# The modulation sums of a two-block layer: partition sums by 64 TensorE transposes, or by VectorE block transposes, column sums and five products

## The reference

```python
silu_c = jax.nn.silu(c)                 # (1, 2048)
silu_cc = jax.nn.silu(c_ctx)            # (2048,)
mod = (silu_c @ w_ada[l] + b_ada[l])    # w_ada: 2048 x 12288
mod_c = silu_cc @ w_ada[l] + b_ada[l]
sh_a, sc_a, gt_a, sh_f, sc_f, gt_f = split(mod, 6)      # 2048 values each
csh_a, csc_a, ...                    = split(mod_c, 6)  # only the first two are used
h  = rms_norm(x, g_attn) * (1 + sc_a) + sh_a            # hc likewise, for the context
x  = x + gt_a * mixer(h, hc)
h  = rms_norm(x, g_ffn) * (1 + sc_f) + sh_f
x  = x + gt_f * swiglu(h, ...)
```

## Time and profile before

| | |
|---|---|
| median of 3 runs | 2425.29 us (2425.19 to 2425.72) |
| profiled execution | 2426.32 us |
| its span, first to last instruction | 2424.6 us |
| mean granted TensorE clock | 0.999 |
| TensorE busy (matmuls) | 2402.5 us, 99% |
| VectorE busy | 1800.6 us, 74% |
| ScalarE busy | 1119.0 us, 46% |
| GpSimd busy | 162.2 us, 7% |
| moved by DMA | 556.93 MB, mean 230 GB/s |

### The profile page before, as it was taken

One profiled execution on the slowest core, in us unless ns is written; L12 is line 12 of the kernel. 1 busy time (PEld: TensorE's weight loads), 2 busy tenths in 40 slices (PEclk: granted clock), 3 DMA queues, 4 the chain that ended last, 5 costly groups with the idle time before them and its releaser, 6 DMA issues.

```text
span 2424.6 us, 28710 instructions
## 1 busy us (share of the span) xinstructions
PE 2402.5 (99%) x11098; PEld 1977.9 (82%) x11098; DVE 1800.6 (74%) x2429; ACT 1119.0 (46%) x1464; POOL 162.2 (7%) x186
## 2 busy tenths in 40 slices
PE   9999999999999999999999999999999999999998
PEld 7888888888888888888788888777788888888887
DVE  5688868888899888788878857677777765555555
ACT  5344444444455454456743333644544443444443
POOL 2010000000000001000011100002000100000000
PEclk9999999999999999999999999999999999999999
DMA  9888766666588668877985656455898976667663
GB/s 303 256 269 273 239 218 195 195 184 195 188 267 267 211 213 292 293 257 255 316 270 186 222 171 233 132 159 177 268 302 283 292 233 193 195 211 227 210 213 124
DMA packets 280100, 556.93 MB, mean 230 GB/s; under 512 B 18503, under 2 KB 23901, under 8 KB 278428
## 3 DMA queue, kind: packets, MB, share of 16 engines
q1 hardware_dynamic: 270588, 515.16, 66.0%
q0 software_dynamic: 9088, 37.85, 5.4%
q10 hardware_dynamic: 288, 2.10, 0.2%
HBM read 543.07 MB, written 15.11 MB: 230 GB/s over the span
## 4 chain that ended last, share of the span: by engine, by line
PE 94%; DVE 3%; issue 1%; ACT 1%; DMA 1%; SPq 0%; POOL 0%; ACTq 0%; POOLq 0%; DVEq 0%
PE pb L2155 92%; PE pb L2159 3%; DVE wlo L1395 1%; DMA raw<-in_w_in 1%; DVE acc L1417 1%; ACT whi L939 0%; DVE sm L1946 0%; DVE x L1774 0%; DVE across L1427 0%; DVE gn L2015 0%; DVE x L1777 0%; DVE x L1495 0%; DVE stz L1497 0%; DVE x L1510 0%; DVE fl L2003 0%
## 5 line engine op out<-in xcount | busy, mean ns | idle before, releaser
L939 ACT ACTIVATE whi<-raw 128x1024 fp32r<-128x1024 f32 (+1 forms) x791 | 828.2, 1049 | 1105.5 <-PE pb L2155 1030.5
L1395 DVE TENSOR_TENSOR wlo<-raw,whi 128x1024 fp32r<-128x1024 f32 (+1 forms) x791 | 958.1, 1218 | 446.8 <-ACT whi L939 444.6
L2155 PE MATMUL pb<-whi,xh 128*128 128x512 f32 (+1 forms) x1184 | 465.1, 393 | 0.7 <-DVE xl L1548 0.7
L2155 PE MATMUL pb<-whi,xl 128*128 128x512 f32 (+1 forms) x1184 | 458.2, 387 | 0.0
L2155 PE MATMUL pb<-wlo,xh 128*128 128x512 f32 (+1 forms) x1184 | 457.6, 386 | 0.0
L1417 DVE SCALAR_TENSOR_TENSOR acc<-raw,silc,acc 128x512 f32<-128x512 f32 x480 | 346.1, 752 | 5.7 <-DMA raw<-in_w_ada 0.7
L2155 PE MATMUL pb<-whi,fh 128*128 128x512 f32 x704 | 274.8, 390 | 1.4 <-DVE fl L2003 1.4
L2155 PE MATMUL pb<-whi,fl 128*128 128x512 f32 x704 | 274.0, 389 | 0.0
L2155 PE MATMUL pb<-wlo,fh 128*128 128x512 f32 x704 | 273.9, 389 | 0.0
L2155 PEld LDWEIGHTS pb<-whi,xh 128*128 128x128 f32 x1184 | 222.6, 188 | 46.6 <-issue 2.9
L2155 PEld LDWEIGHTS pb<-whi,xl 128*128 128x128 f32 x1184 | 222.3, 188 | 46.0
(11 more groups left out here) (426 smaller groups left out, 2828.9 us busy)
## 6 DMA issues: line engine op xcount, KB each, us to landing
raw<-in_w_in SPq DMA_DIRECT2D x375, 512.0 KB, 4.6
raw<-in_w_ada SPq DMA_DIRECT2D x192, 512.0 KB, 4.9
raw<-in_ffn_wg SPq DMA_DIRECT2D x88, 512.0 KB, 4.4
raw<-in_ffn_wu SPq DMA_DIRECT2D x88, 512.0 KB, 4.8
raw<-in_ffn_wd SPq DMA_DIRECT2D x88, 512.0 KB, 4.1
raw<-in_w_branch SPq DMA_DIRECT2D x64, 512.0 KB, 3.9
raw<-in_w_out SPq DMA_DIRECT2D x64, 512.0 KB, 4.4
scr_h<-sil POOLq DMA_DIRECT2D x11, 512.0 KB, 4.0
```

Of the source, the lines that this page charges most:

```text
L939: return eng.activation(dst, src, ACT.Copy)
L1395: tt(wlo[:, u, a:b, 0:n], raw[:, l % NRAW, a:b, 0:n], f32(whi[:, u, a:b, 0:n]), ALU.subtract) \
L2155: return eng.matmul(dst, l, r, start=start, stop=stop)
```

## The change

Each slot is now summed by itself. VectorE transposes `acc[:, slot]` in place in blocks of 32 x 32, so that `acc[32 a + i, 32 j + r]` becomes what stood in partition 32 a + r, column 32 j + i, and reduces over r into 16 columns of a new tile `part` [128, 256]: `part[32 a + i, j]` is the sum over the 32 partitions of quarter a. This is done one beat after the piece's end (`fold`, now a chain of VectorE, ahead of the `ada_end` chains and behind the others), for the second row of pieces 0 to 7 two beats after. The four quarters are added on TensorE by one product with `kfold`, a constant 128 x 128 matrix of 16 unit matrices of 32, which leaves the sum on all four quarters. There are five groups: pieces 0 to 7 (256 columns of `part`), and four times four pieces (64 columns). The product comes six beats after the group's last piece (five for the group of piece 19), and VectorE then picks from each quarter of the PSUM bank every fourth column and adds the bias, in four small ops a group. `across` goes, GpSimd's `fold` goes, and GpSimd loads `kfold` (64 KB) after the rope tables.

```diff
--- before.py
+++ after.py
@@ -111,6 +111,7 @@
         co, si = np.cos(ang), np.sin(ang)
         return np.stack([np.concatenate([co, co], -1), np.concatenate([-si, si], -1)], 1).astype(np.float32)
 
+    c["k_fold"] = np.tile(np.eye(32, dtype=np.float32), (4, 4))
     c["k_rope128"] = rope(128)
     c["k_rope64"] = rope(64)
     return c
@@ -184,7 +185,8 @@
         ident = small("ident", [128, 128])
         par = small("par", [128, 112])
         mod = small("mod", [128, 8, 16])
-        across = small("across", [128, 512])
+        part = small("part", [128, 256])
+        kfold = small("kfold", [128, 128])
         bcol = small("bcol", [128, 96])
         rope_off = small_at[0]
         ropeA = small("ropeA", [128, 2, 2, 128])
@@ -528,8 +530,11 @@
 
 
 
-        pairs = [[(p, 0), (p, 1)] for p in range(8)] + [[(p, 0), (p + 1, 0)] for p in range(8, len(pieces), 2)]
-        pair_of_piece = {p: f for f, pair in enumerate(pairs) for p, _ in pair}
+        groups = [range(8)] + [range(p, p + 4) for p in range(8, len(pieces), 4)]
+
+        def part_of(p, m):
+            rows, n = pieces[p][1], pieces[p][2]
+            return 16 * (4 * rows[m] + n if p < 8 else p - 8)
 
         def sub_done(i):
             s, _, _, end = subs[i]
@@ -593,6 +598,8 @@
         B["h2"] = E["o3"], E["o3"] + 2
         B["gT"] = [ada_beat[11] + 9, ada_beat[23] + 9]
         B["gta"] = B["ot"][7] + 2
+        B["ada"] = [ada_beat[g[-1]] + 6 for g in groups]
+        B["ada"][3] = ada_beat[19] + 5
         B["hid"] = [E[f"fu{s}"] for s in range(11)]
 
         GAP = dict(na=5, gq=4, ml=3)
@@ -736,13 +743,6 @@
                               scr_row.rearrange("h x -> (h x)").partition_broadcast(128)) \
                     .then_inc(*M.inc(S("scr_band"), "scr_band", by=16))
 
-            def fold():
...
-
             def ln_rows(key, b, k, g, bias):
                 yield from until(b)
                 W.wait_ge("exb_free", k - 1)
@@ -770,6 +770,7 @@
                 eng.dma_start(ropeB[:, :, :, :].rearrange("p t a b -> p t (a b)"),
                               I["k_rope64"].rearrange("(t p) a b -> p t (a b)", p=128)) \
                     .then_inc(*M.inc(S("rope_in"), "rope", by=16))
+                eng.dma_start(kfold[:, :], I["k_fold"]).then_inc(*M.inc(S("kfold_in"), "kfold", by=16))
                 for i, n in enumerate(("gqa_gq_2", "gqa_gk_2", "diff_gsub_2")):
                     eng.dma_start(grow[:, i, :], I[n][0].partition_broadcast(128)) \
                         .then_inc(*M.inc(S("grow_in"), "grow", i, by=16))
@@ -917,7 +918,7 @@
                             .then_inc(*M.inc(S("hs_in"), "hs", s, a, by=16))
 
             chains = [start(), na_table(), band_table(), ln_rows("ln_b", B["ln_b"], 1, "sgu_ln_g", "sgu_ln_b"),
-                      ln_rows("ln_d", B["ln_d"], 3, "conv_ln_g", "conv_ln_b"), tables(), attention1(), residual(), fold(),
+                      ln_rows("ln_d", B["ln_d"], 3, "conv_ln_g", "conv_ln_b"), tables(), attention1(), residual(),
                       context(), norm1(), gqa(), mla1(), out2(), gates(), norm2(), hidden(), final(), na_bias(), diff()]
             for i in range(NSUB + 2):
                 beat[0] = i
@@ -1401,10 +1402,11 @@
                 W.wait_ge("raw", l)
                 if x == 0:
                     W.wait_ge("silc")
-                    if pair_of_piece[p]:
-                        W.wait_ge("across", pair_of_piece[p] - 1, 2)
-                        if 1 in slots[p]:
-                            W.wait_ge("ada_sum", pair_of_piece[p] - 1)
+                    for m in range(two):
+                        if 0 < p < 8:
+                            W.wait_ge("folded", p - 1, m)
+                        elif p >= 8:
+                            W.wait_ge("folded", *((7, p - 8) if p < 10 else (p - 2, 0)))
                     if p == 0:
                         W.wait_ge("relT")
                 for k in range(2):
@@ -1417,38 +1419,38 @@
                             ins = stt(a, raw[:, l % NRAW, k, :], c, a, ALU.mult, ALU.add)
                         ins.then_inc(*M.inc(S("ada_acc"), "ada", p, x + k, m))
                 M.value["raw_free", l] = M.value["ada", p, x + 1, two - 1]
-                f = pair_of_piece[p]
...
-                        tt(dst, dst, bcol[:, col:col + 4], ALU.add).then_inc(*M.inc(S("mod"), "mod", r, n))
+
+            def fold():
+                for p in range(len(pieces)):
+                    for m in range(len(pieces[p][1])):
+                        yield from until(ada_beat[p] + 1 + m)
+                        a, k = acc[:, slots[p][m], :], part_of(p, m)
+                        W.wait_ge("ada", p, 15, m)
+                        eng.transpose(a, a).then_inc(*M.inc(S("ada_t"), "turned", p, m))
+                        W.wait_ge("turned", p, m)
+                        if p == 8:
+                            W.wait_ge("ada_sum", 0)
+                        eng.tensor_reduce(part[:, k:k + 16], a.rearrange("p (j r) -> p j r", r=32), AX, ALU.add) \
+                            .then_inc(*M.inc(S("ada_fold"), "folded", p, m))
+
+            def ada_end(g):
+                yield from until(sum_beat[g] + 1)
+                W.wait_ge("ada_sum", g)
+                for a in range(4):
+                    q = slice(32 * a, 32 * a + 32)
+                    if g == 0:
+                        sums = side("ada_sum", g)[q, 0:256].rearrange("p (t c m a) -> p t c m a", t=2, c=2, m=16)
+                        bias = bcol[q, 0:32].rearrange("p (c m) -> p c m", c=2).unsqueeze(1).broadcast_to([32, 2, 2, 16])
+                        dst = mod[q, 0:4, :].rearrange("p (t c) m -> p t c m", t=2)
+                        tt(dst, sums[:, :, :, :, a], bias, ALU.add).then_inc(*M.inc(S("mod"), "modq", g, a))
+                    else:
+                        c0, (r,), _ = pieces[groups[g][0]]
+                        sums = side("ada_sum", g)[q, 0:64].rearrange("p (m a) -> p m a", a=4)
+                        tt(mod[q, r, :], sums[:, :, a], bcol[q, c0 // 128:c0 // 128 + 16], ALU.add) \
+                            .then_inc(*M.inc(S("mod"), "modq", g, a))
+                for p in groups[g]:
+                    for r in pieces[p][1]:
+                        M.value["mod", r, pieces[p][2]] = M.value["modq", g, 3]
 
             def evacuate(s, tb):
                 kind, n, ps = s.evac[0], s.ncols, main_ps(s, tb)
@@ -2111,7 +2113,7 @@
                       *[oT_low("ml", h, B["ml"][h] + 4) for h in range(4)],
                       ot_low(), gates(), norm2(),
                       hidden(), final(),
-                      *[ada_end(f) for f in range(len(pairs))]]
+                      fold(), *[ada_end(g) for g in range(len(groups))]]
             for i in range(NSUB + 2):
                 beat[0] = i
                 for s in strips:
@@ -2491,16 +2493,17 @@
                         W.wait_ge("mod", row, n)
                     tr(ps[0:16, 0:128], mod[:, row, :]).then_inc(*M.inc(S("side"), "gT", r))
 
-            def ada_sum(f):
-                yield from until(ada_beat[pairs[f][1][0]] + 4)
+            def ada_sum(g):
+                yield from until(B["ada"][g])
                 while min(busy.values()) > beat[0]:
                     yield
-                sum_beat[f] = beat[0]
...
-                ins.then_inc(*M.inc(S("side"), "ada_sum", f))
+                sum_beat[g] = beat[0]
+                last = groups[g][-1]
+                W.wait_ge("folded", last, len(slots[last]) - 1)
+                W.wait_ge("kfold")
+                ps = take(("ada_sum", g), ("modq", g, 3), beat[0] + 1)
+                a, n = (0, 256) if g == 0 else (64 * g - 64, 64)
+                mm(ps[:, 0:n], kfold[:, :], part[:, a:a + n]).then_inc(*M.inc(S("side"), "ada_sum", g))
 
             mlw = (("Tc", "mkn", 3), ("Tc", "mqr", 3), ("Tc", "mqn", 3), ("kpT",))
             chains = [small_start(), mixer(), rows_T(("yT", "A"), B["yA"], a_in, ("yl", "A"), ("grp", 3)), sgu(),
@@ -2535,7 +2538,7 @@
                                lambda c, h=h: k4[:, c, h, 128:256], ("oTl", 8 + h), *mlw) for h in range(4)],
                       gates(),
                       h2_T(),
-                      *[ada_sum(f) for f in range(len(pairs))]]
+                      *[ada_sum(g) for g in range(len(groups))]]
             def warm(n):
                 for _ in range(n):
                     mm(banks[NMAIN - 1][:, 0:128], ident[:, :], ident[:, :])
```

More of the change, by code:

```diff
@@ L737, in band_table @@
                     .then_inc(*M.inc(S("scr_band"), "scr_band", by=16))
-            def fold():
-                for f, pair in enumerate(pairs):
-                    yield from until(ada_beat[pair[1][0]] + 1)
-                    W.wait_ge("across", f, 2)
-                    eng.tensor_tensor(acc[:, 1, :], acc[:, 1, :], across[:, :], ALU.add) \
-                        .then_inc(*M.inc(S("folds"), "fold", f))
             def ln_rows(key, b, k, g, bias):
@@ L1419, in ada @@
```

(11 more changed lines are left out.)

23 lines of the change are left out of this document (removed).

## The result

| | before | after |
|---|---|---|
| median of 5 runs each | 2425.19 us (2424.87 to 2425.72) | 2416.5 us (2415.61 to 2417.49) |
| profiled execution | 2426.32 us | 2416.5 us |
| span | 2424.6 us | 2414.8 us |
| mean granted clock | 0.999 | 0.999 |

The ratio is 0.9964, 95% interval 0.9950 to 0.9977: 8.7 us faster, for a forecast of 9.2 us and 2416.1. The span fell by 9.8; the profiled execution of the kernel before lay 1.1 us above its median, that of the kernel after on it, so 8.7 is the gain and 9.8 the sum of what the two traces show.

What follows compares the result with a forecast made beforehand. TensorE bounds the kernel, busy 2402.5 of 2424.6 us. Gains 6.66 + 0.3 - 0.67 + 1.6 + 1.3 = 9.2 us, taken off 2425.29, give 2416.1; range 2413.8 to 2419.8.

Steps and rivals of the forecast that it cites:

- Transposes removed: TensorE's queue: fifteen of the sixteen four-transpose sums go, at 0.44 us each, 6.66 us gained.
- The other price: Skill page's 275 ns for each of 64 transposes on TensorE: 17.5 us, forecast near 2407; not used for the sum.
- rival 4: Some of the 16 transpose blocks on TensorE were free; half of 6.66 would give 2419.4; chance 0.03.
- The small wait for GpSimd: TensorE's smaller wait for GpSimd's fold, at the first one-row pair's sum, goes: 0.3 us gained.
- Products added: Five `kfold` products on TensorE, one of 256 columns and four of 64: 0.67 us lost, ends 0 and 1.1.
- The folds at no cost: VectorE's folds of 1.4 us after the 24 pieces cost TensorE nothing; 4.2 us for three without cover.
- Rival 3: VectorE becomes the bound where already full, folds delaying low halves and raw loads; 2430; chance 0.03.
- The stalled stretch: Piece 19, from 1661.33 to 1665.62: TensorE stands 2.7 us instead of 4.29, 1.6 us gained.
- Rival 2: The stalled stretch's stand doesn't shrink because GpSimd holds up VectorE's ops, fold included; 2419.2; chance 0.13.
- The clock: Behind the stalled stretch, 1666 to 1670: granted clock stays up after the shorter stand, 1.3 us gained.
- rival 1: The clock falls again behind the shorter stand of the stalled stretch; 7.9 us gained, 2417.4; chance 0.2.
- Its later loads issue earlier: nothing there is waited for by TensorE: GpSimd's queue, no longer waiting at the folds, issues its later loads earlier, with no effect on TensorE.

Runs made afterwards that it cites:

- Experiment 2: Changed kernel with four unit-matrix transposes, read by nobody, put back on TensorE at each of the 16 old places; 2423.27 us.
- experiment 5: Changed kernel with GpSimd waiting for VectorE's folds where its adds stood, so its loads issue when they did before; 2415.55 us, ratio 0.9956.
- Experiment 4: Changed kernel with the reduce of every fold done three times; 2422.21 us.
- experiment 8: Changed kernel with the reduce of piece 19's fold alone done five times; 2421.83 us.
- experiment 11: Experiment 5 with the fold of piece 19 two beats later, behind two beats of low halves; 2415.09 us.
- experiment 1: The changed kernel once more, no edit; 2416.88 us, ratio 0.9959.
- Experiment 3: Kernel before with GpSimd's 16 adds done by VectorE, transposes and copies kept; 2428.77 us, ratio 1.001.
- experiment 7: Changed kernel with the reduce of piece 19's fold alone done three times; 2416.11 us.
- experiment 9: Changed kernel with the reduce of piece 19's fold alone done four times; 2420.57 us.
- experiment 12: Experiment 5 again, unchanged, as partner of experiment 11 on the same chip; 2415.26 us, ratio 0.9957.
- Experiment 10: Changed kernel with GpSimd's eight adds of the x2 halves cut to one column of 512; 2415.2 us.
- experiment 6: Experiment 5 with the loads of `w_ada` shifted so that piece 19 ends before strips o0 and o1; 2418.27 us.

## Why the prediction was right, and where it was not

**Transposes removed: right, a little low.** 15 x 0.44 was taken from starts; by beats each is 0.48, since the main steps behind the block stay near 0.24 for a while. 7.2 instead of 6.66. Experiment 2 puts them back and pays the same 0.48. The other price, 275 ns each (the Trainium skill, "TensorE: Matmul & The Clock Gate", "Part 4: PE-mode transpose"), and the estimate of 17.5 us from it, would have been more than twice too much: the trace agrees with it as a duration (274 ns), while the queue time is 0.11 to 0.12. With this fell rival 4: no block was free but the one that stands in the stall.

**The small wait for GpSimd: right.** 0.3 forecast, 0.28 gained at beat 386.

**Products added: the term was mis-sized, and outside its ends.** 0.67 forecast with an upper end of 1.1; measured 0.44 and four times some 0.23, 1.35. The step that failed is the count in the earlier trace rows: I took `x8` and `x12` as so many products. In the trace each product with `kfold`, of plain f32 operands, is two instructions, and the kernel's own loops have four and six products at the places of the earlier trace rows. So the price of one product is double what I divided out. The rows were right; the unit was wrong.

**The folds at no cost: right.** 24 places, and the one loss behind a fold, at beat 329, is gone in experiment 5, which has the same folds. Experiment 4 shows the margin: double length costs 5 us in all. The durations of 0.70 and 0.69 were as read. The forecast of 9 us more busy time on VectorE was wrong (0.8 came), because other work on VectorE got shorter: the low halves fell from 943.3 to 938.8 us, and four other groups by 1 us each. GpSimd's adds, now gone, are the likely reason; no run takes them away alone. That was off the path and changes nothing at the end. Rival 3 had no place to happen.

**The stalled stretch: mechanism right, size off, and part of the gain is luck.** Forecast a stand of 2.7 us; it was 1.30. Two terms of the chain were wrong and nearly cancelled. I let GpSimd delay the two x adds by 0.98 each instead of 0.36; they took 1.07 and 1.08, as before, 1.2 us less in all. The low halves took 2.24 instead of the 1.21 that I had, 1.0 more. From the first evacuation (1650.78) to the end of the first low half (1657.77) are 7.0 us; the forecast had 7.2. So the chain was sized about right, and the stand is shorter because the chain began 1.2 us earlier measured by TensorE.

Nearly all of that is one low half. The pair of low halves ahead of the chain starts 11.4 us before TensorE stops in both kernels, and takes 3.45 us before and 2.35 after. GpSimd's row of adds begins 1.05 us behind the start of the pair before, and 1.20 after. The other traces fall on the same two sides: the pair takes 3.45 where the row begins 1.02 to 1.07 behind its start (experiments 8 and 11), and 2.35 where it begins 1.12 or more behind (experiments 1 to 5, 7, 9 and 12). The second low half starts about 1.1 us behind the first, so it seems to be slow where the row is already running. No run changed this moment on its own: the cause is read from the traces and not shown. With a pair of 3.45 the stand would by estimate (1.30 + 1.10) have been 2.4 us: 1.1 of the 3.0 us by which the stand shrank belong to the moment and not to the change.

Experiment 10 shows what GpSimd's adds do there: without them x add 0.69, low halves 1.2, accumulations at full speed, no stand. Experiment 3 shows that the gain came from less VectorE work and not from GpSimd leaving the chain. That the fold itself is not held up was the step where a rule bore. The Trainium skill, "GPSIMD Engine Reference", "1. Specifications", has contention for VectorE instructions in a two-port mode or with two SBUF inputs. The trace agrees: low halves 2.24 for 1.22 and x add 1.07 for 0.69, both with two SBUF inputs, and transpose and reduce, with one, unchanged at 0.70 and 0.69. The copies, 1.40 for 0.42, have one input too and would have to be of the two-port kind, which no row here tells. Rival 2 fell by the fold's own rows.

**The clock: right in the result, wrong in the reason.** It stayed at 1.00 behind a stand of 1.3 us, as it did behind 1.51 in experiment 7. "A stand of 2.7 us lies between. I take it that the clock stays up" is the step that failed: behind 2.53 us it fell in experiment 9 and cost 1.4. Had the stand been as forecast, rival 1 would by that have come, and with it 2417.4 or a little more. The shorter stand kept the wrong assumption from costing anything: 1.6 + 1.3 = 2.9 forecast, 4.4 gained, of which 1.4 is the shorter stand. A stand of 2.4 us, as without the luck of the moment, lies between 1.51 and 2.53, and no run tells what the clock does there.

**"Its later loads issue earlier: nothing there is waited for by TensorE": wrong.** True of the loads themselves, whose data nobody wants yet. But with 5 MB of them issued at once main loads took 13.2 us instead of 7.1 to land, ScalarE and VectorE were late, and TensorE waited 0.7 us at beat 329. Pacing them again gives it back (main loads 8.6 us), and 0.2 at beat 383. The burst is needed for the loss and is not enough: experiment 3 has the burst, without the folds, and loses nothing; experiment 5 has the folds, without the burst, and loses nothing. What the burst meets in the kernel after, the folds or only another moment, stays open.

**The sum.** Forecast 9.2; span 9.8, median 8.7. Too little by 0.5 (transposes) and 1.7 (stretch, without its product), too much by 0.7 (products) and 0.7 (loads); beat 383, the first two beats and the rest make 0.2 to 0.3 less. The closeness of 2416.1 to 2416.5 is partly luck: four terms were off by 0.5 to 1.7, in both directions, and 1.1 of the largest is the moment of GpSimd's adds.

## What to carry to other kernels

Price side work of a busy TensorE from the starts of the instructions on both sides of it, and find out how many instructions of the trace one call in the code makes before dividing. When a step is taken off an engine, look at what that engine issues next: a wait may have been the pace of its DMAs, and a load that nobody waits for can delay those that someone does. When a gain near a busy stretch is larger than its sum, compare the instructions ahead of the change too: here one of them was shorter by chance. A wait is named after its last semaphore; take that releaser away in thought and see what is late next, as experiment 3 did on the chip.

## What the hardware showed that was not expected

- A product of plain f32 operands counts as two instructions, and both must be paid: 0.44 us for 256 columns and 0.23 for 64, in a queue where a product of 512 columns with fp32r weights steps at 0.227. By column that is four times the price at 256 columns and eight times at 64.
- Beside GpSimd's adds VectorE is slower by kind of instruction: 3.3 times (copies of 64x512), 2.3 times (accumulations of 128x512), 1.8 times (low halves of 128x1024), 1.5 times (128x512 adds from SBUF), 1.0 (block transposes, reduces, and the evacuation `sg<-gta,pb` at 0.67). With 39 us of GpSimd's adds gone, VectorE's busy time grew by 0.8 and 2.3 us in two executions, where the instructions removed and added make 10.
- The granted clock fell behind stands of 2.53 and 4.26 us that followed and preceded full work (0.59 and 0.50, at a price of 1.4 and 2.3 us), and did not behind 1.30 and 1.51. In experiment 6 it fell to 0.65 behind a wait of 2.44 us that followed shorter ones.
- Two executions of the same program differ by 1 us in one stand (1.30 and 0.25, experiments 5 and 12). The last two accumulations ahead of it took 3.47 us in one and 2.44 in the other. GpSimd's adds began ahead of these accumulations in the first and beside them in the second.
